# The first FFN's first units computed from scaled, unshifted inputs, with the shifts added as small products and a bias

## What is computed

```python
def modulated_norm(h, w, mod, i):
    return rmsnorm(h, w) * (1.0 + mod[:, :, 3 * i + 1]) + mod[:, :, 3 * i]
def swiglu(y, w_up, w_down):
    a, b = jnp.split(y @ w_up, 2, axis=-1)
    return (jax.nn.silu(a) * b) @ w_down
...
mod_x = adaln_params(c, w_mod[l], b_mod[l])      # silu(c) @ w_mod + b_mod, 9 sections of 1024
mod_c = adaln_params(c_ctx[None], w_mod[l], b_mod[l])
x = ffn_sublayer(x, mod_x, 0, norm_w[l, 0], ffn1_w_up[l], ffn1_w_down[l])
ctx = ffn_sublayer(ctx, mod_c, 0, norm_w[l, 0], ffn1_w_up[l], ffn1_w_down[l])
```

## Time and profile before

| what | us |
|---|---|
| three runs | 2147.23, 2147.34, 2145.22 |
| their median | 2147.23 |
| the profiled execution, whole | 2148.09 |
| its span, first to last instruction | 2146.3 |
| PE busy in that span | 2132.3 |

### The profile page before, as it was taken

The page is one execution under the profiler, slowest core; times in us unless marked ns, Lnnn a source line. Parts: engine busy times, 40 slices in busy tenths (PEclk is TensorE's granted clock), DMA queues, the critical chain, the costliest instruction groups (busy, mean ns, idle before and its releaser), DMA issues.

```text
span 2146.3 us, 26126 instructions
## 1 busy us (share of the span) xinstructions
PE 2132.3 (99%) x10615; PEld 1803.9 (84%) x10615; DVE 1402.1 (65%) x1919; ACT 776.9 (36%) x1147; POOL 0.2 (0%) x4
## 2 busy tenths in 40 slices
PE   8999999999999999999999999999999999999998
PEld 6888888988888888888888888888889888888887
DVE  5677777646588873477777767633335678677764
ACT  4322222443322222342222233222223555556653
POOL 0000000000000000000000000000000000000000
PEclk9999999999999999999999999999999999999999
DMA  8655555341455553345555544433333537765664
GB/s 260 196 167 172 160 168 161 124 118 39 124 162 157 177 157 98 89 143 162 176 167 159 168 133 147 135 93 97 98 91 106 157 97 199 205 197 148 187 188 144
DMA packets 454394, 318.12 MB, mean 148 GB/s; under 512 B 10478, under 2 KB 429702, under 8 KB 453894
## 3 DMA queue, kind: packets, MB, share of 16 engines
q1 hardware_dynamic: 432476, 243.43, 39.2%
q10 hardware_dynamic: 21800, 73.03, 10.0%
HBM read 312.23 MB, written 1.05 MB: 146 GB/s over the span
## 4 chain that ended last, share of the span: by engine, by line
PE 97%; SPq 1%; DVE 1%; DMA 1%; ACT 0%; issue 0%
PE bank L620 23%; PE bank L622 23%; PE bank L621 23%; PE bank L618 9%; PE bank L619 5%; PE bank L899 4%; PE bank L651 2%; PE bank L932 1%; PE bank L655 1%; PE bank L687 1%; PE bank L685 1%; PE bank L686 1%; SPq L543 1%; PE bank L804 1%; PE bank L913 1%; DMA RAW<-in_ffn_w_up_dram 1%
## 5 line engine op out<-in xcount | busy, mean ns | idle before, releaser
L1461 DVE TENSOR_TENSOR LO<-RAW,HI 128x1024 fp32r<-128x1024 f32 (+1 forms) x435 | 523.3, 1207 | 351.6 <-ACT HI L1028 351.3
L620 PE MATMUL bank<-Y,HI 128*128 128x512 f32 (+1 forms) x1440 | 555.7, 386 | 0.0
L622 PE MATMUL bank<-Y,LO 128*128 128x512 f32 (+1 forms) x1440 | 553.6, 384 | 0.0
L621 PE MATMUL bank<-Y,HI 128*128 128x512 f32 (+1 forms) x1440 | 553.5, 384 | 0.0
L1028 ACT ACTIVATE HI<-RAW 128x1024 fp32r<-128x1024 f32 (+1 forms) x435 | 441.7, 1039 | 119.4 <-DVE MODACC L1472 34.9
L620 PEld LDWEIGHTS bank<-Y,HI 128*128 128x128 f32 x1440 | 270.6, 188 | 54.2 <-issue 1.2
L622 PEld LDWEIGHTS bank<-Y,LO 128*128 128x128 f32 x1440 | 270.6, 188 | 53.7
L621 PEld LDWEIGHTS bank<-Y,HI 128*128 128x128 f32 x1440 | 270.6, 188 | 53.6 <-issue 0.5
L1472 DVE SCALAR_TENSOR_TENSOR MODACC<-MODRAW,SC,MODACC 128x1024 f32<-128x1024 f32 x224 | 277.2, 1279 | 2.4 <-DMA MODRAW<-in_w_mod_dram 2.0
L618 PE MATMUL bank<-Y,HI 128*128 128x512 f32 x720 | 254.0, 398 | 0.0
L620 PE MATMUL bank<-Z,HI 128*128 128x512 f32 (+1 forms) x594 | 218.0, 367 | 0.0
(11 more groups left out here) (255 smaller groups left out, 2379.0 us busy)
## 6 DMA issues: line engine op xcount, KB each, us to landing
RAW<-in_ffn_w_up_dram SPq DMA_DIRECT2D x174, 512.0 KB, 3.9
MODRAW<-in_w_mod_dram ACTq DMA_DIRECT2D x128, 512.0 KB, 4.4
RAW<-in_w_in_dram SPq DMA_DIRECT2D x128, 512.0 KB, 4.1
RAW<-in_ffn_w_down_dram SPq DMA_DIRECT2D x66, 512.0 KB, 4.0
RAW<-in_ffn_w_down_dram SPq DMA_DIRECT2D x24, 384.0 KB, 3.5
WM<-in_w_mod_dram SPq DMA_DIRECT2D x16, 512.0 KB, 8.7
RAW<-in_w_ret_out_dram SPq DMA_DIRECT2D x16, 512.0 KB, 4.5
RAW<-in_w_conv_out_dram SPq DMA_DIRECT2D x16, 512.0 KB, 4.6
```

The source lines that it names most:

```text
L620: mm(bank, hi, X[:, k, 0, cols], start=first, stop=False)
L621: mm(bank, hi, X[:, k, 1, cols], start=False, stop=False)
L622: return mm(bank, lo, X[:, k, 0, cols], start=False, stop=end)
L1461: V_.tensor_tensor(weights(v, 1), raw_weights(v), weights(v, 0).bitcast(F32), ALU.subtract).then_inc(lo_done, 1)
```

## The change

The pieces of w_mod come in another order: all four groups of the scale (WM0 to WM7) first, then all four of the shift (WM8 to WM15), with the weights of units 0 to 4 after each of the first five pairs. ACT writes XN times AMUL in place, then its high part YP (`scaled_hi`), DVE the low part (`scaled_low`); `first_units` multiplies units 0 to 3 with YP instead of Y. When shifts arrive, `mods0` splits them into SH (high and low part, two token kinds each). `shifts(g)` on PE multiplies the two blocks of group g of each of the four units with SH: HI by four columns, LO by two, all into bank 4. At the end DVE copies the sums out (FXP) and adds them to FX, the shift's share in each output channel. Silu takes FX as its bias, and DVE's product adds it, each in two halves since latent and context differ. Unit 4 (`fifth_unit`) is multiplied in the same stage with the true Y, which `y0` on ACT and `y0_low` on DVE still make, now from the scaled XN. `unit_done` for units 0 to 3 is signalled by `shifts(3)`. Units 4 and 5 use banks 6 and 7. Core of the diff:

```diff
@@ plan
-            s.rows = [[p.acc(4), p.acc(5)] for g in range(4)]
-            s.cols_acc = [[p.acc(6), p.acc(7)] for g in range(4)]
+            s.rows = [p.acc(4 + (i % 2 if i < 5 else 1)) for i in range(8)]
+            s.cols_acc = [p.acc(6 + i % 2 if i < 4 else 7) for i in range(8)]
+            s.fix_acc = p.acc(4)
@@ SPq
-                        g, sec, k0 = b // 4, 1 - b % 4 // 2, 4 * (b % 2)
+                        g, sec, k0 = b // 2 % 4, 1 - b // 8, 4 * (b % 2)
...
+                    for i in range(5):
+                        load_mod(2 * i)
+                        load_mod(2 * i + 1)
+                        load_up(i)
+                    for b in range(10, 16):
                         load_mod(b)
@@ PE
+                    def shifts(g):
+
+                        if g == 0:
+                            bank_wait(pe, s.fix_acc)
+                        pe.wait_ge(sh_done, g + 1)
+                        for cc in range(4):
+                            for k in (2 * g, 2 * g + 1):
+                                mm(B[4][:, 4 * cc:4 * cc + 4], HI[cc][:, k * P:(k + 1) * P], SH[:, k, :],
+                                   start=(k == 0 and cc == 0), stop=False)
+                                ins = mm(B[4][:, 4 * cc:4 * cc + 2], LO[cc][:, k * P:(k + 1) * P], SH[:, k, 0:2],
+                                         start=False, stop=(k == KT - 1 and cc == 3))
+                            if g == 3:
+                                ins.then_inc(unit_done, 1)
...
-                    columns(0, 1)
+                    columns(0)
                     drain_wait(pe, s.turn[6])
-                    keep_clock(5, s.turn[6].bank)
+                    keep_clock(8, s.turn[6].bank)
+                    drain_wait(pe, s.turn[7])
+                    first_units((0, 1), (0,))
+                    modulation(1)
+                    keep_clock(4, s.turn[7].bank)
+                    columns(1)
+                    first_units((0, 1), (1,))
+                    first_units((2, 3), (0, 1))
                     modulation(2)
-                    keep_clock(3, s.turn[6].bank)
+                    keep_clock(4, s.turn[7].bank)
+                    columns(2)
+                    first_units(range(4), (2,))
                     modulation(3)
...
+                    first_units((4, 5), (0,))
+                    columns(3)
+                    first_units((4, 5), (1, 2))
+                    first_units(range(6), (3,))
                     modulation(4)
+                    first_units((6, 7), (0,))
+                    columns(4)
+                    first_units((6, 7), (1, 2, 3))
                     modulation(5)
...
+                    shifts(0)
+                    fifth_unit((0, 1))
+                    columns(5)
                     modulation(6)
+                    shifts(1)
+                    fifth_unit((2, 3))
+                    columns(6)
                     modulation(7)
...
+                    shifts(2)
+                    fifth_unit((4, 5))
+                    columns(7)
+                    shifts(3)
+                    fifth_unit((6, 7))
@@ ACT
+                    def scaled_hi(*ks):
+                        act.wait_ge(mods0_done, ks[-1] // 2 + 1)
+                        for k in ks:
+                            act.wait_ge(xn_done, k + 1)
+                            for h, cs in enumerate(HCOLS):
+                                A(XN[:, k, 1, cs], XN[:, k, 1, cs], ACT.Copy, scale=AMUL[:, h, k:k + 1]).then_inc(xa_done, 1)
+                        for k in ks:
+                            act.wait_ge(xa_done, 2 * k + 2)
+                            A(yp(k, 0), XN[:, k, 1, :], ACT.Copy).then_inc(yp_hi, 1)
...
+                            if follows_ada(s) and cc < 4:
+                                act.wait_ge(fx_done, 1)
+                                for h, cs in enumerate(HCOLS):
+                                    ins = A(TMP[:, o % 2, cs], B[s.acc[cc].bank][:, cs], ACT.Silu, bias=FX[:, cc, h:h + 1])
@@ DVE, end of ada
+                    mods0(4)
+                    split_upto(4)
+                    y0_low(0, 1)
+                    for i in range(5, 8):
+                        mods0(i)
+                        y0_low(2 * i - 8, 2 * i - 7)
+                    dve.wait_ge(unit_done, 4)
+                    V_.tensor_copy(FXP[:].rearrange("p c n -> p (c n)"), B[4][:, 0:16]).then_inc(drained[4], 1)
+                    drain_wait(dve, s.fix_acc)
+                    V_.tensor_tensor(FX[:], FXP[:, :, 0:2], FXP[:, :, 2:4], ALU.add).then_inc(fx_done, 1)
```

More of the change, by code:

```diff
@@ L213, in plan @@
                 totals(s.u + c, 1)
-                s.acc.append(p.acc(c % (8 if s.wide else 4)))
+                s.acc.append(p.acc(c + 2 if at == 1 and c < 6 else c % (8 if s.wide else 4)))
         elif s.kind == "q":
@@ L485, in bank_wait, with yp @@
                 eng.wait_ge(drained[acc.bank], acc.use - 1)
+        def yp(k, part):
+            return YP[:, (k + 4) % KT, part, :]
         def unit_words(u):
@@ L563, in _ @@
                     w = UP[s.which][s.layer]
-                    for cc in range(0 if s.halves else 4, s.n):
+                    for cc in range(0 if s.halves else 5, s.n):
                         load(s.u + cc, block_of(w, 0, KT, (cc // 2) * P + (cc % 2) * FF))
@@ L807, in first_units @@
-                            for cc in units:
-                                ins = mm(B[cc][:], HI[cc][:, k * P:(k + 1) * P], Y[:, k, 1, :],
-                                         start=False, stop=(k == KT - 1))
-                                if k == KT - 1:
-                                    ins.then_inc(unit_done, 1)
+                            pe.wait_ge(yp_lo, k + 1)
+                            for cc in units:
+                                mm(B[cc][:], HI[cc][:, k * P:(k + 1) * P], yp(k, 1), start=False, stop=(k == KT - 1))
@@ new lines, in fifth_unit @@
+                    def fifth_unit(ks):
+                        u, acc = up_s.u + 4, up_s.acc[4]
+                        if 0 in ks:
+                            bank_wait(pe, acc)
+                            pe.wait_ge(lo_done, u + 1)
+                        for k in ks:
+                            pe.wait_ge(y0_hi, 2 * k + 2)
+                            pe.wait_ge(y0_lo, k + 1)
+                            ins = block_mm(B[acc.bank][:], u, k, Y, k, up_s.cols, k == 0, k == KT - 1)
+                        if KT - 1 in ks:
+                            ins.then_inc(unit_done, 1)
@@ L831, in _ @@
                     modulation(0)
-                    drain_wait(pe, s.turn[0])
-                    keep_clock(3, s.turn[0].bank)
-                    modulation(1)
                     bank_wait(pe, s.rb_acc)
@@ L860, in _ @@
-                    for b in range(8, 12):
-                        modulation(b)
-                    first_units((3,), (2, 3))
-                    columns(2, 1)
-                    columns(2, 0)
-                    for b in range(12, 16):
-                        modulation(b)
-                    first_units((4,), range(4))
-                    columns(3, 1)
-                    columns(3, 0)
-                    first_units((5,), range(4))
-                    first_units((6, 7), (0, 1))
@@ L882, in _ @@
                         first_four(s, before.kind == "out", between)
-                    for cc in range(4, s.n):
+                    for cc in range(5 if before.kind == "ada" else 4, s.n):
                         unit(s, cc, s.acc[cc], Y)
```

215 lines of the change are left out of this document (98 added, 117 removed).

## The result

The changed kernel takes **2165.49 us** (median; 2164.10 to 2167.98), the kernel before 2147.02 in the runs beside it. The ratio is 1.0089, with a 95% interval of 1.0077 to 1.0101: slower by 18.5 us, where 15.3 were forecast. The median lies inside the range of 2157 to 2170, but 0.5 us above the band that I gave the forecast itself (2161 to 2165), at the foot of the band of the rival "the clock falls more often". The profiled execution took 2164.11 us, 16.0 more than that of before; it is one of the two shortest of the four.

The account below looks back on a forecast made before the run. PE bounds the kernel, so only unit 5's start counts: 20.9 + 27.2 + 6.5 + 3.1 + 2.2 + 1.1 + 7.0 + 8.5 + 3.3 = 79.8 against 64.5, 15.3 later. Forecast 2162.5 against the median, range 2157 to 2170.

Parts of the forecast that it names:

- the forecast itself: Whole kernel: unit 5 starts 15.3 us later, the time lands at 2161 to 2165; chance 0.45.
- the clock falls more often: Rival, chance 0.22: clock reads half in the shift stretches too, loads cost up to 7.0 more, unit 4 up to 4: 2165 to 2175.
- first product of unit 0: Start of PE's products, once YP of block 0 and LO of unit 0 exist: at 20.9, 2.1 earlier than before.
- changes of form: PE switching back to products or to shifts before unit 5: eleven, 1.1 us.
- keep_clock, two: Two keep_clock(4) between products ahead of columns on PE: 8 x 0.27 = 2.2 us, covered by nothing.
- 64 shift products: Small products with SH for units 0 to 3: 0.11 each, 7.0 us, all on PE.
- (a): Behind columns(1), PE waits for unit 1's LO, which DVE splits only after MODS and AMUL: 1.8 us.
- (b): Behind columns(2), the same wait for unit 2's LO: 1.8 us.
- wait (c): Behind columns(7), only shifts(3) can run and needs MODS and two tiny operations for SH: 0.8 us.
- wait (d): Before unit 5: FX, table load, Silu, HI, LO take 5.1 to 5.2 from shifts(3); 1.4 covered, PE waits 3.8.
- clock before unit 5: Granted clock falls twice behind PE's gaps, surely the long one and one other, 1.65 once, 3.3 us together.
- 0.3 for Y operands: PE waits for the Y operands of blocks 2 and 3: 0.3 us within the 8.5 of waits.

Follow-up runs that it names:

- experiment 7: Changed kernel with the edits of experiment 4 and experiment 5 together and the modulations' banks exchanged: 2157.80 us.
- (6): Changed kernel without the two keep_clock(4) behind modulation(1) and modulation(2): 2166.77 us.
- experiment 2: Kernel before with 64 small products added, four at a time between wide products, results unused: 2155.10 us.
- experiment 3: Changed kernel with only 7 of its 64 shift products left, every wait kept: 2163.20 us.
- (8): Kernel of experiment 7 with only 7 of its 64 shift products left: 2153.06 us.
- experiment 5: Changed kernel with HI and LO of units 1 to 3 split before the modulation's rows and columns are waited for: 2160.64 us.
- experiment 4: Changed kernel with unit 5's weights split and the Silu table loaded ahead of the wait for FX: 2161.85 us.
- 9: Kernel of experiment 7 with shift products in rows of eight, each ahead of three wide products, instead of sixteen ahead of six: 2164.18 us.
- experiment 1: Kernel before with 64 small products added in a row ahead of the last products of units 0 to 3, results unused: 2158.38 us.

## Why the prediction was right, point by point

The sign, the place and the size in the profile held: unit 5 at 79.99 instead of 79.8. The median came 3.0 us above the forecast of 2162.5. By its steps (numbers in brackets in the last column are the experiments):

| step | forecast | profile of after | what it is worth by the runs |
|---|---|---|---|
| first product of unit 0 | 20.9 | 22.23 | 0.5 of it the bank (7) |
| modulation, each | 0.93 | 1.00 | |
| changes of form | 1.1 | 1.7 | |
| keep_clock, two | 2.2 | 2.0 | 0 (6) |
| 64 shift products | 7.0 | 7.2, and 0.3 at the low clock | 7.1 added to before (2); 57 of them 1.6 to 1.7 taken from after (3), 2.8 to 4.9 from the mended one (8) |
| waits (a), (b), from the end of columns | 1.8 + 1.8 | 1.8 + 1.8 (idle in the rows: 1.63 each) | 3.1 to 4.1 with the clock (5) |
| wait (c) | 0.8 | 0.66 | |
| wait (d), from shifts(3) to unit 5 | 5.1 to 5.2 | 5.11 | 2.9 (4) |
| clock before unit 5 | 3.3 | 1.6 + 0.3 | |
| clock behind unit 5's start | 0 | 2.0 | |

**The start was too early by 1.3, in three parts.** Modulation(0) now writes the bank of the input transposes that ACT empties with its third copy, before it was the second; the idle before it is 1.50 instead of 1.0, and giving the old bank back brings 1.01 (experiment 7). Counted from ACT's second table load, which takes the scatter of the start out, modulation(0) comes after 6.5 us in the five traces with the new bank and after 6.0 in the seven with the old one. The diff has this in one line, `s.rows`, and my steps never asked which bank comes free when. From ACT's second table load at 7.62 (7.08 in the earlier trace rows) another 0.5 is a later start of that execution, the scatter named above. The last 0.25 lies between the end of LO (21.98) and the first product, for which I had nothing.

**The waits** are the best part: each was a chain of named operations with durations from rows, and (a) to (d) came within 0.15 as lengths of chain. The idle time that I gave for (d), 3.8, didn't: the row has 2.20, since the six products ahead of it ran at the slow clock and filled more of the chain. The 0.3 for Y operands didn't come at all. (a) and (b) carry "issue" as releaser, but experiment 5, which moves only the split, removes them.

**The shift products** cost what the nearest row said, 0.111 each (58.90 to 60.71 for sixteen). The 25 ns that the Trainium skill ("TensorE: Matmul & The Clock Gate", section Back-to-back issue gap) gives as the floor for narrow matmuls would have made, by an estimate, 1.6 us of them; the trace doesn't bear that out for products that each load their own weights. But I wrote "all on PE", and as a statement of what they are to blame for it is wrong: behind them stands the chain row copy, columns, MODS, Y high, Y low, and without the products PE waits 2.9 us for it in three stretches (experiment 3).

**The table load:** the Silu follows 1.30 after the load's start (75.51, 76.81). The drain of 1.38 that the Trainium skill adds ("ScalarE: Activation LUTs", section What ACT_TABLE_LOAD costs) isn't there, nor is it in experiment 4, where ACT works up to the load (74.91) and its next operation starts 1.29 behind it; by it, an estimate, unit 5 would have started 1.4 later, near 81.4.

**The clock is the step that was mis-sized.** Two falls came in the profiled execution, as forecast; that it was two is in part luck, since experiments 3 and 4 had one more in the sweep with the same code there. I had priced both at 1.65. The first cost eight products at 0.427 instead of 0.227, 1.6. The second lasted 10.2 us instead of 3.4. Up to unit 5 it cost 0.3, since the slowed products lay under wait (d), which is a chain of ACT and DVE; behind it ten products of unit 5 took 0.2 more each, 2.0 that no term of mine had. The rival "the clock falls more often" named the shift stretches, and is partly true: in experiments 5 and 9 the fall begins within one, with no wait ahead of it in 5 and one of 0.2 us in 9. But the first three shift stretches of after ran at 1.00 (58.9 to 74.0). My rule that it follows a gap was too narrow; experiment 1 shows a fall with PE busy throughout.

**The ends.** 15.5 at unit 5 and 2.2 behind it, 2.0 of them the clock, make the 17.7 at unit 7. The two profiles differ by only 16.0 at the end, since 1.7 is won back in the last wide stage by a pace that isn't the kernel's (below). The medians differ by 18.5, 3.2 more than forecast: 2.2 of these are the part behind unit 5, where I had nothing; the rest can't be placed from one profile. That unit 5 was met to 0.2 owes much to errors that cancel: 1.3 too little for the start, 1.1 for modulations and changes of form and 0.2 for the shift products, against 1.4 too much for the clock before unit 5, 0.3 for Y operands that never waited, and 0.7 in the rest (columns, keep_clocks, waits).

**Why the change loses.** It removes waits of the sweep for shifts, 2.2 us, which were there for other reasons. It adds 7.2 us of products, a modulation and columns more behind the first product, two keep_clocks, and sets unit 5 behind a chain of 5.1. Mending its waits gives 7.7 back; at least 10.7 stayed in every version tried that still computes the shifts.

## What to carry to other kernels

The small products cost their full time when added to the busiest engine, but taking them out of another order gave only what the next chain left, so measure both. One profile shows one execution: compare distances between events and not starts, and don't credit an edit with a fall of the clock that came or stayed away once. When a kernel rearranges accumulators, ask for each bank which copy empties it and when, also at the start. Price a stretch of narrow matmuls twice, by their starts and by the clock that is granted in and behind them, because the slow clock outlives the stretch and then slows the wide products.

## What the runs showed of the hardware that I had not expected

The granted clock can fall while PE is busy: in a row of 64 narrow products, 0.111 us apart, it went from 1.00 to 0.51, with 5.2 us of the row and 18 us of gapless other work ahead of it; the same 64 in fours between wide products left it at 1.00 for 16 us; among eights, modulations and columns it was 0.50 for 20.5 us. And with the same code it fell in one execution and not in another: from 34.5 to 38 us it was 0.53 in before and 0.52 in experiment 2, but 1.00 in experiment 1.

The pace of one and the same stage varies from one execution to the next at full clock. In the last wide up stage pairs of 512 and 256 columns fill PE in both kernels. Twenty us of it in the profiles of before, of after, and of experiment 3, which has the code of after in that stage:
```profile
2000.00:2020.00 20.00, 20.00 (x115) 17.32 (x114) 14.34 (x23) 12.20 (x21) 0.00 (x0) 1.00 0.64 188
```
```profile
2020.00:2040.00 20.00, 20.00 (x118) 17.62 (x117) 14.13 (x24) 12.12 (x22) 0.00 (x0) 1.00 0.66 195
```
```profile
2000.00:2020.00 20.00, 20.00 (x115) 17.35 (x114) 15.16 (x24) 12.34 (x24) 0.00 (x0) 1.00 0.64 185
```
115 products or 118 in the same time. From unit 7 on both kernels execute the same 10170 products. Up to the last thousand the distances agree to 0.2 us; in the last thousand, more than half of them in this stage, after is 2 us faster, and so the two profiled spans mislead by 1.7. The traces of experiments 1 and 5 have the fast pace too. What sets it stayed open.
